# Placing a matmul kernel's SBUF operands by 256 bytes instead of 128, and moving some work of the expert layers and the merge

## The reference, cut to what matters

```
q = (t @ w_query).reshape(t_count, 8, 2, 128)
s1, i1 = top_k(scores of half 0, 16);  s2, i2 = top_k(scores of half 1, 16)
top_s, pos = top_k(s1[:, None] + s2[None, :], 16)
idx = take(i1 * 128 + i2, pos);  gate = softmax(top_s)
out = sum_k  gelu(expert_u[idx_k] . t) * gate_k * expert_v[idx_k]
```

## Time and profile before

| | |
|---|---|
| profiled execution | 4009.23 us |
| its span | 4007.9 us |
| granted TensorE clock, mean | 0.969 of 2.4 GHz |
| TensorE matmul busy | 3803.1 us |
| VectorE, ScalarE, GpSimd busy | 2650.6, 1589.6, 1003.4 us |
| HBM traffic | 544 MB read, 102 MB written |

### The profile page before, as it was taken

The page is one execution under the profiler, slowest core; times in us unless marked ns, Lnnn a source line. Parts: engine busy times, 40 slices in busy tenths (PEclk is TensorE's granted clock), DMA queues, the critical chain, the costliest instruction groups (busy, mean ns, idle before and its releaser), DMA issues.

```text
span 4007.9 us, 60163 instructions
## 1 busy us (share of the span) xinstructions
PE 3803.1 (95%) x24424; PEld 3302.1 (82%) x24424; DVE 2650.6 (66%) x5092; ACT 1589.6 (40%) x2370; POOL 1003.4 (25%) x476
## 2 busy tenths in 40 slices
PE   7988999999999999999999999998999999988799
PEld 5667988788888888778888888698999999978799
DVE  3794554389677777367766665778774678766575
ACT  3323454332344444321111113554665333447454
POOL 1334553235433333300000000068666000000000
PEclk8999999899999999999999998999999999998899
DMA  5340000224445554666776653056678788742255
GB/s 192 105 142 6 1 1 1 68 82 141 142 160 182 181 180 162 230 226 227 249 243 226 226 194 90 15 169 202 222 255 276 249 277 272 238 155 85 85 169 169
DMA packets 222723, 650.53 MB, mean 162 GB/s; under 512 B 20080, under 2 KB 89584, under 8 KB 214640
## 3 DMA queue, kind: packets, MB, share of 16 engines
q1 hardware_dynamic: 116224, 401.92, 32.1%
q10 hardware_dynamic: 106224, 244.77, 17.1%
HBM read 544.38 MB, written 101.71 MB: 161 GB/s over the span
## 4 chain that ended last, share of the span: by engine, by line
PE 80%; DVE 7%; DMA 5%; ACT 4%; POOL 2%; issue 1%; ACTq 0%; POOLq 0%; SPq 0%; DVEq 0%
PE ps L133 78%; DMA ring<-in_v 3%; DVE lo L80 2%; PE ps L136 2%; POOL lo L80 2%; ACT hi L128 2%; DVE g_b L80 1%; DMA ring<-in_gdn_in 1%; DVE cond L113 1%; ACT L124 1%; DVE g_acc L92 0%; ACT n_s L125 0%; ACT g_b L124 0%; DMA pcA<-pcga 0%; ACTq L75 0%
## 5 line engine op out<-in xcount | busy, mean ns | idle before, releaser
L80 POOL TENSOR_TENSOR lo<-ring,hi 128x1024 fp32r<-128x1024 f32 x328 | 822.9, 2515 | 1920.9 <-ACT hi L128 1920.8
L128 ACT ACTIVATE hi<-ring 128x1024 fp32r<-128x1024 f32 x725 | 768.3, 1060 | 1115.1 <-PE ps L133 824.6
L80 DVE TENSOR_TENSOR lo<-ring,hi 128x1024 fp32r<-128x1024 f32 (+1 forms) x397 | 485.5, 1224 | 309.1 <-ACT hi L128 308.1
L133 PE MATMUL ps<-pahh,hi 128*128 128x512 f32 x1152 | 469.4, 407 | 12.0 <-POOL lo L80 9.1
L133 PE MATMUL ps<-pahl,hi 128*128 128x512 f32 x1152 | 456.7, 396 | 0.0
L133 PE MATMUL ps<-pahh,lo 128*128 128x512 f32 x1152 | 456.7, 396 | 0.0
L80 DVE TENSOR_TENSOR paone<-ps,paR 128x512 bf16<-128x512 f32 x512 | 329.3, 685 | 153.3 <-PE ps L133 148.9
L133 PE MATMUL ps<-pchh,hi 128*128 128x256 f32 x1152 | 335.1, 291 | 22.3 <-POOL lo L80 20.5
L133 PE MATMUL ps<-pchh,lo 128*128 128x256 f32 x1152 | 326.5, 283 | 0.0
L133 PE MATMUL ps<-pchl,hi 128*128 128x256 f32 x1152 | 326.5, 283 | 0.0
L133 PEld LDWEIGHTS ps<-pahh,hi 128*128 128x128 f32 x1152 | 218.8, 190 | 57.5 <-POOL lo L80 10.2
(11 more groups left out here) (454 smaller groups left out, 9152.7 us busy)
## 6 DMA issues: line engine op xcount, KB each, us to landing
ring<-in_u SPq DMA_DIRECT2D x256, 512.0 KB, 3.7
ring<-in_v SPq DMA_DIRECT2D x256, 512.0 KB, 4.4
paA<-paga ACTq DMA_DIRECT2D x128, 256.0 KB, 2.7
paG<-paR ACTq DMA_DIRECT2D x16, 2048.0 KB, 7.7
paAg<-paA ACTq DMA_DIRECT2D x16, 2048.0 KB, 8.5
paGg<-paG ACTq DMA_DIRECT2D x16, 2048.0 KB, 16.7
late_w<-in_adat ACTq DMA_DIRECT2D x56, 512.0 KB, 3.7
ring<-in_ffn_up SPq DMA_DIRECT2D x44, 512.0 KB, 3.9
```

What stands on the lines that cost most here:

```text
L80: return Op(self.e.tensor_tensor(out, a, b, op) if self.real else None)
L128: return Op(self.e.activation(out, a, ACT.Copy, scale=scale) if self.real else None)
L133: return Op(self.e.matmul(out, l, r, start=start, stop=stop, skip_group_check=skip) if self.real else None)
```

## The change

Five things are changed.

1. `place` is taken modulo 256, and the three places become 224, 224 and 160. The tensor at `hi` was at 224 modulo 256 before as well.
2. `equal` compares with a copy of `iota` in PSUM (`i_ps`, bank 3), which is made before the decoding instead of after it; in layer 1 the float indices `ixf`, which `times` multiplies by, lie in PSUM too (bank 2).
3. In layer 1 the gates start behind tile 38 instead of 36, behind five tiles of every six instead of four of five. The last group is then behind tile 114 instead of 115.
4. In layer 1 the fetch is seven tiles behind the last group instead of four: at tile 121 instead of 119.
5. In the merge, ScalarE calls `hi_to(out[0])` after the high half of block 1, and VectorE `lo_to(out[0])` after block 2 of y.

```
@@ class Memory, alloc
-            at += (place - at) % 128
+            at += (place - at) % 256
@@ issue
-    WEIGHT, WIDE, NARROW = 96, 96, 32
+    WEIGHT, WIDE, NARROW = 224, 224, 160
@@ peer_up
-        ixf = scr(256 * nt).rearrange("p (t n k) -> p t n k", t=nt, n=16)
+        ixf = scr(256 * nt) if nt == 4 else bank[2][:, :]
+        ixf = ixf.rearrange("p (t n k) -> p t n k", t=nt, n=16)
...
-        spread = (1, 2) if nt == 4 else (1, 1, 1, 1, 0)
-        many = {i: spread[i % len(spread)] for i in range(turn_at + 2, 128)}
+        start = turn_at + 2 if nt == 4 else turn_at + 4
+        spread = (1, 2) if nt == 4 else (1, 1, 1, 1, 1, 0)
+        many = {i: spread[i % len(spread)] for i in range(start, 128)}
         behind, n_groups = {}, w // 4
-        for i in range(turn_at + 2, 128):
+        for i in range(start, 128):
...
-        fetch = last + 4
+        fetch = last + 4 if nt == 4 else last + 7
@@ peer_up, vector, behind the top-k
+            dve.cp(i_ps, iota).then_inc(s_pick, (name, "iota"))
             dve.cp(top, tv[:, :, :, 0].rearrange("p t h -> p (t h)")).then_inc(s_pick, (name, "top"))
...
-            i16 = iota[:, 0:16].unsqueeze(1)
+            i16 = i_ps[:, 0:16].unsqueeze(1)
...
-            dve.cp(i_ps, iota).then_inc(s_pick, (name, "iota"))
-            dve.wait_ge(s_pick, (name, "iota"))
@@ merge, scalar
                     act.cp(yp[0][:, m, :], y[:, m, :]).then_inc(s_yh, m)
+                    if m == 1:
+                        hi_to(out[0])
@@ merge, vector
                     if m:
                         low(m - 1)
+                    if m == 2:
+                        lo_to(out[0])
```

## The result

The changed kernel takes 3962.99 us (median of four runs, 3952.61 to 3968.50), the kernel before beside it 4012.61 (4007.65 to 4022.31): 49.6 us less, ratio 0.9865 with a 95% interval of 0.9845 to 0.9885. The forecast was 70 us less than 4013.7, or 3944: 20 of the 70 did not come. The profiled execution of the changed kernel took 3968.5 us (span 3967.1), 40.7 us less than the profiled one before; it is the slowest of its four.

What follows compares the result with a forecast made beforehand. TensorE, 80% of the chain of waits, was taken to bound the kernel. Terms 43 + 1 + 10 + 7.5 + 5 + 7.5 = 74 us, shaved to 70, take 4013.7 to 3944 us; range 3880 to 3992.

Steps and rivals of the forecast that it cites:

- Part 1: Operand places modulo 256: 512-column matmuls in layer 0 and gdn gain 6.0 ns each, 43 us; the merge's pairs 1 us.
- The 227 ns: Spacing forecast for 512-column matmuls with operands level, in place of 233.0 ns; taken as twice 113.3.
- The projection, where I counted half: Gdn's projection: 768 matmuls of 512 columns, counted as 384 at 6.0 ns because it has stalls of its own.
- most of the stall goes: First rival: level places free 512-column reads of 16 ns or more of 19.7; 3869 us, chance 0.15.
- no account: Second rival: place does not matter for 512 columns, only parts 2 to 5 are left; 3984 us, chance 0.27.
- the bad place: Third rival: level makes 512-column weight loads and moving reads meet, spacing over 237 ns; 4048 us at 9 ns, chance 0.10.
- Part 2: Layer 1's decoding: PSUM inputs return GpSimd's lo subtractions to 2.39 us, ending TensorE's waits; net 10 us.
- The 1.5 us that I took off: Layer 1's decoding: deduction because spacing is 113.3 ns after a stall but tends to 117.8 without one.
- Part 3: Layer 1's gates two tiles later: TensorE's 6.2 us wait for first columns and half clock behind it go; 7.5 us.
- Part 4: Layer 1's later fetch: ScalarE's 3.2 us store wait goes, loads and spill stall fewer remaining tiles; 5 us.
- Part 5: Merge: third w_out2 tile split earlier, TensorE's 12.6 us gap falls to 4 to 5 us; gain 7.5 us.
- The fourth rival: Level places help, but parts 3 and 4 give nothing as the columns' wait moves to the fetch; 3957 us, chance 0.08.

Runs made afterwards that it cites:

- no_places: The changed kernel with the three places as before (modulo 128: 96, 96, 32), all other parts kept: 3994.6 us, ratio 0.9939.
- decoding_only: The kernel before with only the copy of iota and the float indices in PSUM during the decoding: 4001.3 us, ratio 0.9959.
- split loads: The changed kernel with layer 1's gates from tile 40 and the second pair of four loads issued behind the last spill, both layers: 3934.2 us, ratio 0.9799.
- gates40_only: The changed kernel with layer 1's gates from tile 40 (six tiles of seven), the four loads kept together: 3952.2 us, ratio 0.9827.
- both_moved: The changed kernel with weights and every pair moved by 128 bytes (places 96, 96, 32 modulo 256), distances kept: 3952.1 us, ratio 0.9837.

## Why the prediction was right, and where it was not

The direction, the range and the largest part held; the sum was 74 us and the parts measure some 54. Three of the five parts came as worked out or near it; two did not, and as they were small and the range 112 us wide, the time fell inside it all the same. That is no evidence for those two.

**Part 1: right in kind, 43 forecast, 36 measured.** The 227 ns were right to 0.6 ns in the chains (227.3 to 227.6), but by luck: the reason for the value, twice the 113.3 of the earlier trace rows, does not hold as a mechanism, since level gives 120 at 256 columns, not 113. Why level is the good place at 512 columns is open. The mis-sized term is the count times 6.0: in the down product 3072 matmuls gave 716 - 699 = 17 us in the chain against 18.4, but in the query and up products, with the norm, the scores and the gates between them, the mean distance of two starts went from 232.5 to 227.8 ns, 4.7 in place of 6.0, and the stage from 929.1 to 914.8 us, 14.3 against 20.7 (16.6 from no_places to the changed kernel). The merge's pairs, 1 us forecast, show none of it in the changed kernel: `hmp` and `on` stay at 117.8 ns. The projection, where I counted half, gives 255.2 us in the mean of eight kernels with level places against 259.1 of five without: 3.9 us, about 768 x 5 ns, but no pair of traces shows it, as single runs lie up to 6.5 us from those means. The three rivals on the place (most of the stall goes, no account, the bad place) have fallen by 698 to 699 us against 716. The third was wrong only for 512 columns: level is the bad place for 256. And of the second this much is true: among the other places tried, 512 columns take 232.4 to 233.3 ns at each.

**Part 2: right, 10 forecast, 11 to 12 measured.** GpSimd came back to 2.40 us, VectorE's operations to 2.28. The 1.5 us that I took off, because without stalls the spacing tends to 117.8, has the wrong reason: decoding_only runs tiles 1 to 32 at 113.4 without a stall, so a stall does not decide which of the two values comes.

**Part 3: wrong, 7.5 forecast, 1.6 measured.** The failed step is "two tiles or 5.7 us later: 6.2 - 5.7 leaves 0.5 us". It took the time at which the columns are ready as fixed. That time depended on the wait: the earlier trace rows show columns made while TensorE, and so GpSimd, stood still. Without the wait VectorE met GpSimd twice more and delivered 4.3 us later. The half clock behind the wait stayed with it.

**Part 4: wrong in sign, 5 forecast, -2.4 to -4.3 measured.** The removed wait was real (3.2 us). What I mis-sized is "the stall they cause falls on the last tiles, with fewer tiles left to be hit". A spill behind the four loads took 16.1 us in place of 14.15, and ScalarE, waiting for it, split no tile in the meantime; with the fetch at tile 121 that wait ended 8.4 us ahead of the down product's first matmul, in the kernel before 14.0 us ahead of it, so there was less time left to catch up: fewer tiles behind the stall made it dearer, not cheaper. The split loads show that the queue is the cause: with half the bytes ahead of the spills, the longest wait for one is 5.1 us in place of 10.1, and the turn 6.8 us shorter.

**Part 5: right, 7.5 forecast, 8.2 measured** (31.6 us earlier before the merge's turn, 39.8 behind it; 7.4 to 9.2 by pairs of the table), with the gap at 4.4 us as forecast.

The fourth rival (parts 3 and 4 give nothing, 3957 us) is nearest to what happened, for another reason than the one given for it and together with the 7 us missing from part 1; it had a chance of 0.08. I treated two schedule changes as differences of fixed times, and both times were set by what they were to replace.

## What to carry to other kernels

In a stream of matmuls like this one, each with a load of weights of its own, lay the moving operand and the weights out by their distance modulo 256, by width, and read the spacing per width from a chain without waits: a place that is best at 512 columns can be the worst at 256. When a wait is to be hidden by doing other work first, ask whether the awaited work runs beside something that the wait had kept quiet. And put only what is needed next ahead of small stores with a deadline in one queue: splitting four loads into two pairs was worth 19 to 20 us by the stages, more than any other edit of the schedule here.

## What the runs showed that I had not expected

At 256 columns, 64 bytes below the weights, the spacing has two values, 113.4 and 118 ns, in the same kernel, with the same tensors at the same places: the MLP's stage up to its down product takes 127.0 to 128.3 us in eight of the kernels above and 132.1 to 132.5 in three, two of them with the places of before, one with those of the change. The decoding's stretch above shows the same. In all kernels with these places the value holds from one pause of TensorE to the next, over as many as 983 matmuls, and changes only where a start comes late. What chooses is open.

Three of the kernels (those with the gates from tile 40 and level places) compute the norm behind layer 0's down product in less time than the changed one, with nothing edited in it; what gates40_only changes comes later. TensorE pauses 1.59 us ahead of it in all four. The window of it in the changed kernel and in the one with split loads: 17.8 us busy at a granted clock of 0.61, and 10.8 busy for the same 80 matmuls at 1.00. From the first matmul of the norm to the first of the attention it is 21.7 us in the changed kernel, 15.2 in these three, and 20.8 to 22.6 in all others. These 6.5 us came or did not come from one kernel to the next, and why is open; they are part of why gates40_only lies 11 us under the changed kernel with a gain of 8 to show for its edit. That both_moved lies 11 us under it too, with no edit but the places, this does not explain; the intervals of the two overlap, and by stages it is quicker in others (the hybrid's projection and attention take 236.0 us, in the changed kernel 244.3), which range from 235 to 245 us over all the kernels, whatever was edited.

```profile
2396.00:2415.00 19.00, 17.80 (x80) 16.31 (x78) 8.52 (x18) 6.90 (x11) 0.00 (x0) 0.61 0.09 28
```

```profile
2384.00:2396.00 12.00, 10.80 (x80) 9.81 (x78) 7.13 (x18) 6.71 (x11) 0.00 (x0) 1.00 0.15 44
```
